# Subtractions of the "up" weight pieces moved from VectorE to GpSimd in a two-layer mixture-of-experts stage

## The reference, cut to what matters

```python
def expert_block(args):
    xblk, e = args
    h = jax.nn.silu(xblk @ w_gate[e]) * (xblk @ w_up[e])
    return h @ w_down[e]
```

## Time and profile before

| | us |
|---|---|
| median of 3 runs (3621.12 to 3622.97) | 3622.37 |
| the profiled execution | 3624.69 |
| its span | 3623.0 |
| TensorE busy in the span | 3018.1 (83%) |
| VectorE busy | 1924.9 (53%) |
| ScalarE busy | 1080.0 (30%) |
| GpSimd busy | 307.5 (8%) |

### The profile page before, as it was taken

The page is one execution under the profiler, slowest core; times in us unless marked ns, Lnnn a source line. Parts: engine busy times, 40 slices in busy tenths (PEclk is TensorE's granted clock), DMA queues, the critical chain, the costliest instruction groups (busy, mean ns, idle before and its releaser), DMA issues. The chain is left out here.

```text
span 3623.0 us, 35330 instructions
## 1 busy us (share of the span) xinstructions
PE 3018.1 (83%) x13366; PEld 2402.9 (66%) x13366; DVE 1924.9 (53%) x2792; ACT 1080.0 (30%) x1840; POOL 307.5 (8%) x472
## 2 busy tenths in 40 slices
PE   4979988698898798989986499939898998648993
PEld 3757866586776676766875378737676687536882
DVE  3653344342466544655543488744465554347884
ACT  2340130211343112151001277611215100136773
POOL 0020030000342001210000000010121000000001
PEclk8989999789799899989997699969998999769996
DMA  2222202123601131202224399723120222438993
GB/s 84 81 64 82 93 20 82 49 76 113 267 5 53 65 105 58 82 4 70 93 93 153 142 369 405 308 99 105 58 82 4 70 93 93 153 140 313 408 406 125
DMA packets 152240, 467.66 MB, mean 129 GB/s; under 512 B 15598, under 2 KB 29833, under 8 KB 126729
## 3 DMA queue, kind: packets, MB, share of 16 engines
q1 hardware_dynamic: 142712, 431.34, 33.1%
q0 software_dynamic: 9360, 34.08, 2.4%
HBM read 413.49 MB, written 51.90 MB: 128 GB/s over the span
## 5 line engine op out<-in xcount | busy, mean ns | idle before, releaser
L156 DVE CAST weights_r<-weights 128x1024 fp32r<-128x1024 f32 (+4 forms) x270 | 228.6, 847 | 818.5 <-DMA weights<-in_w_in 314.2
L149 PE MATMUL ps<-x_cols_hi_r,weights_r 128*128 128x512 f32 x896 | 361.6, 404 | 48.3 <-DVE weights_r L158 48.3
L158 DVE TENSOR_TENSOR weights_r<-weights,weights_r 128x1024 fp32r<-128x1024 f32 (+4 forms) x270 | 385.9, 1429 | 9.3
L150 PE MATMUL ps<-x_cols_lo_r,weights_r 128*128 128x512 f32 x896 | 357.4, 399 | 0.0
L151 PE MATMUL ps<-x_cols_hi_r,weights_r 128*128 128x512 f32 x896 | 357.1, 399 | 0.0
L149 PEld LDWEIGHTS ps<-x_cols_hi_r,weights_r 128*128 128x128 f32 x896 | 170.4, 190 | 95.2 <-DVE weights_r L158 53.0
L957 POOL TENSOR_SCALAR weights<-weights,weight 128x256 f32<-128x256 f32 (+3 forms) x304 | 151.7, 518 | 728.9 <-DVE weight L851 435.1
L901 ACT ACTIVATE weights<-weights,minus_top 128x256 f32<-128x256 f32 (+3 forms) x304 | 167.0, 551 | 146.9 <-DVE minus_top L814 146.9
L150 PEld LDWEIGHTS ps<-x_cols_lo_r,weights_r 128*128 128x128 f32 x896 | 170.8, 191 | 42.4 <-issue 1.4
L151 PEld LDWEIGHTS ps<-x_cols_hi_r,weights_r 128*128 128x128 f32 x896 | 170.5, 190 | 41.6
L149 PE MATMUL ps<-hawk_xT_hi_r,weights_r 128*128 128x512 f32 x384 | 155.1, 404 | 25.3 <-DVE weights_r L158 25.3
(11 more groups left out here) (475 smaller groups left out, 6902.9 us busy)
## 6 DMA issues: line engine op xcount, KB each, us to landing
weights<-in_w_in SPq DMA_DIRECT2D x64, 1024.0 KB, 5.3
raw_pieces<-in_w_exp_down SPq DMA_DIRECT2D x46, 1024.0 KB, 8.2
raw_pieces<-in_w_exp_up SPq DMA_DIRECT2D x36, 1024.0 KB, 7.6
weights<-in_w_exp_gate SPq DMA_DIRECT2D x34, 1024.0 KB, 7.0
raw_pieces<-in_w_exp_gate SPq DMA_DIRECT2D x32, 1024.0 KB, 7.4
weights<-in_w_exp_up SPq DMA_DIRECT2D x30, 1024.0 KB, 7.4
weights<-in_hawk_w_in SPq DMA_DIRECT2D x28, 1024.0 KB, 5.2
weights<-in_w_exp_down SPq DMA_DIRECT2D x20, 1024.0 KB, 8.2
```

The source lines that it names most:

```text
L149: pe.matmul(out, as_r(left[1]), as_r(right[0]), start=start, stop=False)
L150: pe.matmul(out, as_r(left[0]), as_r(right[1]), start=False, stop=False)
L156: dve.tensor_copy(as_r(hi), lo).then_inc(rounded, 1)
L158: dve.tensor_tensor(as_r(lo), lo, as_r(hi).bitcast(F32), ALU.subtract).then_inc(done, 1)
```

## The change

The subtraction of the up pieces, for the 15 written-out experts, is made by GpSimd and no longer by VectorE, and counted in a new semaphore `split_up`. TensorE waits on `split_up` for up pieces and on `split`, with the numbers of the others alone, for gate and down pieces. The loop over the late blocks stays as it was. On GpSimd the two subtractions of expert b+1 stand ahead of the wait and the DMA that store expert b's output.

```diff
+    others = [job for job in order if job[1] not in UP]
...
+            def wait_split(b, p):
+                if p in UP:
+                    pe.wait_ge(s.split_up, 2 * (b - 1) + (p - 1))
+                else:
+                    pe.wait_ge(s.split, others.index((b, p)) + 1)
+
...
             split_pieces(1, GATE)
-            split_pieces(1, UP)
             split_pieces(2, GATE)
...
                 hidden(s.hidden_done)
-                if b < LAST:
-                    split_pieces(b + 1, UP[:1])
                 dve.wait_ge(s.h_rounded, b)
                 split_h(s.h_split)
-                if b < LAST:
-                    split_pieces(b + 1, UP[1:])
                 if b + 2 < N_EXPERTS:
                     split_pieces(b + 2, GATE)
...
+            def split_up(b):
+                for p in UP:
+                    pool.wait_ge(s.rounded, at[b, p] + 1)
+                    lo = raw[room[b, p]]
+                    pool.tensor_tensor(as_r(flat(lo)), flat(lo), as_r(flat(hi[p])).bitcast(F32), ALU.subtract).then_inc(s.split_up, 1)
+
+            split_up(1)
             for b in range(1, N_EXPERTS):
+                if b < LAST:
+                    split_up(b + 1)
                 pool.wait_ge(s.out_taken, 2 * b)
                 pool.dma_start(rows_at(moe.y_rows, MAX_OVER + b), ye[:, :]).then_inc(s.y_stored, 16)
```

More of the change, by code:

```diff
@@ L2234, in experts @@
     at = {job: n for n, job in enumerate(order)}
+    others = [job for job in order if job[1] not in UP]
     LAST = N_EXPERTS - 1
-    names = ("x_loaded", "rounded", "split", "used", "x_turned", "x_rounded", "x_split", "silu_done", "hidden_done", "h_turned",
+    names = ("x_loaded", "rounded", "split", "used", "x_turned", "x_rounded", "x_split", "silu_done", "hidden_done", "h_turned", "split_up",
              "h_rounded", "h_split", "out_taken", "y_stored")
@@ L2345, in gate @@
                     pe.wait_ge(s.silu_done, b - 1)
-                pe.wait_ge(s.split, at[b, p] + 1)
+                wait_split(b, p)
                 project(xT[side(b)], p, room[b, p], gate_bank, s.used)
```

## The result

| | us |
|---|---|
| kernel before, median of 4 runs (3621.12 to 3624.05) | 3622.67 |
| changed kernel, median of 4 runs (3659.19 to 3671.47) | 3665.61 |
| ratio, with its 95% interval | 1.0118 (1.0097 to 1.0139) |
| profiled execution of the changed kernel, its span | 3669.82, 3668.1 |

The change makes the kernel 43 us slower (by the interval 35 to 50); 38 were forecast, to 3660. The first lines of the profile show who does the work now: GpSimd has gone from 307.5 us busy to 626.4, while VectorE has lost only 37 of its 1924.9, although 60 subtractions of 2.2 us were taken off it. The rest has become waiting that is recorded as work.

What follows compares the result with a forecast made beforehand. TensorE was taken as the full engine, with hidden on VectorE having no slack. Two layers of 11.5 (ring) plus 7.7 (start) made 38.4 us, 3660.8 from the median of 3622.37, stated as 3660; range 3621 to 3700.

Steps and rivals of the forecast that it cites:

- One GpSimd subtraction, 4.63 us: Each 128x2048 up subtraction on GpSimd was taken to last 4.63 us, with bounds of 4.20 and 4.80.
- B: GpSimd's second up subtraction of an expert, directly after the first: 4.63 us, holding VectorE's gate splits until it ends.
- the ring: Per expert, GpSimd's two up subtractions, then VectorE's gate splits, x, down splits: 19.06 us instead of 18.105.
- Turns by whole instructions: GpSimd and VectorE operations with two SBUF inputs exclude each other for a whole instruction; 2.71 us against 0.69 undisturbed.
- A: GpSimd's first up subtraction of an expert, starting behind VectorE's second down split and ending 4.47 us later.
- The margin of A, 0.57: In steady state A is asked for 0.57 us after the second down split has started, so the order holds.
- Rival 1: A gets in between the down splits in every second expert; 3740 to 3765 us; chance 14%.
- The start, 7.7 a layer: At each layer's start, gate 2, x 2 and hidden of expert 2 come late, with a clock loss: 7.7 us.
- so nothing is lost there: At a layer's start, up 1 on GpSimd ends near when TensorE wants its pieces: no loss.
- The clock term, 1.7: At each layer's start, TensorE's longer wait for hidden keeps its clock longer at the 1.2 GHz level: 1.7 us.
- The sum, 38.4: Over both layers, the ring's 11.5 and the start's 7.7 us, taken twice, add 38.4 us.
- Rivals 2 and 3: Rival 2: A also holds hidden, 3748 us, chance 4%. Rival 3: the subtractions don't exclude each other, 3622, 12%.

Runs made afterwards that it cites:

- up1_only: Kernel before with only the second up piece of each expert subtracted on GpSimd, the first left on VectorE; 3637.79 us, ratio 1.0030.
- no_read: Changed kernel with each GpSimd subtraction replaced by two and a half zero fills of the same room, reading nothing; 3627.5 us, 0.9999 of the kernel before.
- up0_only: Kernel before with only the first up piece of each expert subtracted on GpSimd, the second left on VectorE; 3625.37 us, ratio 0.9996.
- start_on_dve: Changed kernel with both up pieces of expert 1 back on VectorE, all others on GpSimd; 3649.35 us, 1.0060 of the kernel before.
- after_out_later: Changed kernel with ScalarE taking expert b-1's outputs behind the rounding of b's down pieces, not ahead of it; 3658.44 us, 1.0093 of the kernel before.

## Why the prediction was right, point by point

- **One GpSimd subtraction, 4.63 us.** Measured 4.62 alone (up1_only) and 4.63 to 4.66 for B in the ring; writing fp32r cost nothing that shows over the 4.63 worked out from float32 rows. The Trainium skill (GPSIMD Engine Reference, "Elementwise — side-by-side cycle accounting") gives 4.497 us; the trace says 4.62, and by the page's figure the ring would have come out at 18.8. (For the result that is 24 rounds of 0.27 us, some 7 us with the start, a little less than the 8 of the prediction.)
- **Turns by whole instructions.** Right, and for the reason given: no_read and up0_only show that reading beside a two-operand split is what costs. hidden and h ran beside A and were not lengthened (at most 0.68 and 0.69 us in the whole trace, as before). For x the steady state shows nothing: B has ended before it starts. The Trainium skill (SBUF — State Buffer, "Who interferes with whom") states this as a port that the two share and lock for an instruction; the trace agrees, 7.76 us for two gate splits against 4.49.
- **The ring, 19.06.** Measured 19.00, and 11.5 us for its twelve rounds: from the split of x 3 to that of x 15 it takes 2353.54 - 2124.82 = 228.72 us, against 2326.64 - 2109.38 = 217.26 before.
- **The margin of A, 0.57.** A is ready at 2148.49, and the second down split begins at 2145.70 + 2.20 = 2147.90: 0.59. Rival 1 (A between the down splits) is seen at the start only, where it was forecast, and there in the second layer alone: GpSimd asked at 3331.20, 0.46 us after the first down split had begun. In the first layer A had begun at 2102.71, 0.11 us ahead of that split (2102.82), was not held (4.57 us) and held both. The price was the same, 8.8 us for the two down splits:

```profile
3330.74 8.83 DVE L2491 TENSOR_TENSOR raw_pieces_r<-raw_pieces,expert_hi_r 128x2048 fp32r<-128x2048 f32 x2
```

```profile
3331.20 6.22 POOL L2553 TENSOR_TENSOR raw_pieces_r<-raw_pieces,x_cols_lo_r 128x2048 fp32r<-128x2048 f32 x1 [5.93 <-ACT x_cols_lo_r L2392]
```

- **The start, 7.7 a layer.** 7.1 until x 3 ((2124.82 - 2109.38) less the 2082.14 - 2073.84 = 8.30 by which this execution was late on arrival), but its terms were wrong in both directions. Hidden is 2112.28 - 2097.11 - 8.30 = 6.9 us late, not 5.4. The sentence "so nothing is lost there" failed: I had GpSimd begin when up 0 was rounded, and it stood behind its own wait for the landing of the late loop's last store (released by that DMA at 2088.19, some 1.7 us later). TensorE then waited 1.48 us for up 1, a wait that the sum lacked, and gate 2 and x 2 came later by as much. The clock term, 1.7, was put too high: it took a longer stretch at half speed for a longer loss. But the stretch began inside the wait, 3.7 us before TensorE had work (as did the one at 2073.40 before, whose wait ended at 2076.28), so of 6.8 us at half speed TensorE was busy only 3.17, against 3.40 of 3.4 before, and from hidden to x 3 only 0.3 us were added.
- **The sum, 38.4.** In the profiled executions the stage takes 18.6 us more in the first layer and 18.9 in the second (from 3310.38 to 3581.88, against 3282.29 to 3534.90), together 37.5. The executions differ by 45.1: 8.3 us arose before gate 1 of the first layer, 1.2 between the layers, and - 1.9 at the end. The 8.3 do not go with the change. The changed kernel was late in both its profiles (gate 1 at 2082.14 and 2079.79, against 2073.84), but no_read, as fast as the kernel before, reached gate 1 at 2082.13 too, and start_on_dve and after_out_later, both slower, at 2072.37 and 2074.36. Which stretch before the stage differs each time I did not settle. The - 1.9 at the end are the change: the end takes 86.2, 86.5 and 86.3 us in the two profiles of the changed kernel and in start_on_dve, against 88.1 before and 88.2 in no_read. Of this 1.1 us is the shorter way from x to hidden, which the sum left out. Counted from gate 1 to hidden of expert 14, the stages are 17.5 and 17.8 us longer, 35.3 together.
- **How much of the number is luck.** The mechanism gives 35 to 37.5 us by the profiles, the sum had 38.4, and the medians differ by 42.9 and 40.3. That 38.4 lies in both intervals (35 to 50, 32 to 45) says little, for they are wide, and terms of the start that were too small and too large cancelled in part. What bears the account out is the spacing, the members of the ring and the runs that take it apart.
- **Rivals 2 and 3.** Hidden held by A: refuted by its 0.68 us. No exclusion: refuted by the gate splits.

What stays open: why executions reach the stage at times that differ by up to 10 us, and whether the change adds something outside the two stages. The profiles show no such part, but the medians, 40 and 43 us apart, leave room for one.

## What to carry to other kernels

Before moving work to an idle engine, ask what the bounding engine waits for: here it never waited for the pieces that were moved, so the move could give nothing, and all that was left was its price. Two engines that read SBUF in turns form a ring whose length is the sum of their turns; add it up through one period and compare it with the period of the bounding engine, 18.1 us here, since the cost starts where the sum passes it. Splitting the slow engine's instruction did not shorten that sum (19.12 us against 19.00); placing it where the other engine takes an operand from PSUM kept it out of the other's way (A alone cost nothing).

## What the runs showed of the hardware that I had not expected

- A GpSimd subtraction that waited for its turn was recorded as busy in the wait: 4.62 us alone, 5.33 and up to 6.3 in the records. So its busy time was not its work; its uncontended duration has to be taken from a place where it stands alone.
- Filling SBUF from GpSimd (4.71 us a piece, same place) left VectorE's splits as they were: 2293 ns for a gate split against 2284 before.
- At the turn of the two engines the one that waited went first even in the middle of a series: the halves alternated with the two gate splits one for one.
- TensorE's waits of 0.9 us an expert left its granted clock at 1.00 for 245 us; in the wait of 6.3 us (from 2105.98 on) it fell at 2108.6, and it was at half speed for 6.8 us, 3.2 of them busy. Before the change two waits of 1.76 and 1.99 us, with 3.0 us of work between them, were followed by 3.4 us at half speed, all of them busy.
